# Inverse roots of the wide norms as exp(-ln/2) on ScalarE

## The reference

```
first block
  h = rmsnorm(x, norm_mix)                               ("mix")
  p = h @ w_in -> RWKV-7 (8 heads of 64), MLA (8 heads), differential attention (4 heads), gates
  RWKV:  kk = k*k_k / max(||k*k_k||, 1e-12) per head;  y = (y - mean) * rsqrt(var + 64e-5) per head
  MLA:   rmsnorm(c_q) over 256 ("q"), rmsnorm(c_kv) over 128 ("kv")
  diff:  rmsnorm(o, subln, eps=1e-5) over 128, per head   ("dsum")
  x = x + (gated sum of the three branches) @ w_o
  x = x + conv_ffn(rmsnorm(x, norm_ffn))                 ("ffn")
  x = rmsnorm(x, norm_final)                             ("fin")
second block, layers 0 and 1, modulated by silu(c) @ ada_w
  h = h + swiglu(modulate(rmsnorm(h)))                   ("s00", "s10")
  h = h + mixer(modulate(rmsnorm(h)))                    ("m0", "m1"; attention and a gMLP)
  h = h + swiglu(modulate(rmsnorm(h)))                   ("s01", "s11")
return rmsnorm(h, final_g)                               ("out")
rmsnorm(x, g) = x * rsqrt(mean(x*x) + 1e-6) * g
```

## Time and profile before

| | |
|---|---|
| three runs | 3799.27, 3800.09, 3807.25 us; median 3800.09 |
| profiled execution | 3798.57 us, its span 3796.8 us |
| busy, share of the span | PE 91%, PEld 72%, DVE 52%, ACT 34%, POOL 3% |
| granted clock of PE, mean | 0.955 |

### The profile page before, as it was taken

One profiled execution on the slowest core, in us unless ns is written; L12 is line 12 of the kernel. 1 busy time (PEld: TensorE's weight loads), 2 busy tenths in 40 slices (PEclk: granted clock), 3 DMA queues, 4 the chain that ended last, 5 costly groups with the idle time before them and its releaser, 6 DMA issues.

```text
span 3796.8 us, 46184 instructions
## 1 busy us (share of the span) xinstructions
PE 3445.9 (91%) x19472; PEld 2717.1 (72%) x19472; DVE 1960.4 (52%) x3248; ACT 1302.6 (34%) x2247; POOL 105.5 (3%) x202
## 2 busy tenths in 40 slices
PE   6888868999999899998789899999999878889998
PEld 4767736877888688866556688878887645677887
DVE  4665676667666665555544533343334454444333
ACT  3231456434434322224333322232223434333222
POOL 0000000010000011000000000000000000000000
PEclk8999979999999999999899999999999979999999
DMA  3010101454444365522011222222222200122221
GB/s 127 25 56 3 48 34 52 165 195 149 150 155 150 106 238 200 193 102 81 23 36 65 78 95 98 97 83 95 96 98 106 92 23 34 56 84 89 100 94 67
DMA packets 100543, 364.03 MB, mean 96 GB/s; under 512 B 11632, under 2 KB 11696, under 8 KB 99696
## 3 DMA queue, kind: packets, MB, share of 16 engines
q1 hardware_dynamic: 75888, 272.14, 19.8%
q0 software_dynamic: 24448, 88.95, 6.8%
HBM read 358.94 MB, written 2.10 MB: 95 GB/s over the span
## 4 chain that ended last, share of the span: by engine, by line
PE 80%; DVE 14%; ACT 4%; issue 1%; DMA 0%; DVEq 0%; POOL 0%; ACTq 0%; POOLq 0%
PE ps_run L397 79%; DVE wl L1660 1%; DVE nrm L1667 1%; PE ps_run L678 1%; DVE nP L1664 1%; DVE nrm L1670 1%; ACT nP L1021 1%; ACT wh L1021 1%; ACT nrm L1021 1%; DVE HL L1667 1%; DVE nst L1664 1%; DVE sq L1670 1%; DVE nst L2291 1%; ACT L1021 0%; DVE dP L1660 0%
## 5 line engine op out<-in xcount | busy, mean ns | idle before, releaser
L397 PE MATMUL ps_run<-HH,wh 128*128 128x512 f32 x2800 | 1137.9, 406 | 91.2 <-DVE HL L1667 48.9
L397 PE MATMUL ps_run<-HL,wh 128*128 128x512 f32 x2800 | 1109.2, 396 | 0.0
L397 PE MATMUL ps_run<-HH,wl 128*128 128x512 f32 x2800 | 1108.2, 396 | 0.0
L1660 DVE TENSOR_TENSOR wl<-st,wh 128x1024 fp32r<-128x1024 f32 x511 | 625.6, 1225 | 788.1 <-ACT wh L1021 787.6
L1021 ACT ACTIVATE wh<-st 128x1024 fp32r<-128x1024 f32 x511 | 538.3, 1054 | 749.5 <-PE ps_run L397 737.9
L397 PEld LDWEIGHTS ps_run<-HH,wh 128*128 128x128 f32 x2800 | 536.9, 192 | 231.1 <-DVE HL L1667 70.7
L397 PEld LDWEIGHTS ps_run<-HH,wl 128*128 128x128 f32 x2800 | 537.3, 192 | 115.7
L397 PEld LDWEIGHTS ps_run<-HL,wh 128*128 128x128 f32 x2800 | 538.9, 192 | 111.9 <-issue 6.9
L397 PE MATMUL ps_run<-AH,wh 128*128 128x512 f32 x1040 | 408.5, 393 | 0.0
L397 PE MATMUL ps_run<-AH,wl 128*128 128x512 f32 x1040 | 406.4, 391 | 0.0
L397 PE MATMUL ps_run<-AL,wh 128*128 128x512 f32 x1040 | 406.4, 391 | 0.0
(11 more groups left out here) (392 smaller groups left out, 3351.1 us busy)
## 6 DMA issues: line engine op xcount, KB each, us to landing
st<-wst SPq DMA_DIRECT2D x511, 512.0 KB, 3.2
mb<-ada POOLq DMA_DIRECT2D x144, 512.0 KB, 4.3
cw<-cw POOLq DMA_DIRECT2D x4, 1024.0 KB, 6.2
X<-xT SPq DMA_DIRECT2D x8, 256.0 KB, 10.0
X<-xT POOLq DMA_DIRECT2D x8, 256.0 KB, 5.4
out<-X SPq DMA_DIRECT2D x8, 256.0 KB, 2.1
kc<-kc POOLq DMA_DIRECT2D x1, 1137.5 KB, 7.3
mb<-cond POOLq DMA_DIRECT2D x2, 512.0 KB, 5.2
```

What stands on the lines that cost most here:

```text
L397: i = self.e.matmul(out, lhsT, rhs, start=start, stop=stop, skip_group_check=True)
L1660: self.e.tensor_tensor(out, a, b, op).then_inc(*self.w.done(*points))
```

## The change

The root and the reciprocal of every wide norm become two ScalarE instructions: Ln, which reads the sums from the bank with scale 1/dim and the epsilon as a bias, and Exp with scale -1/2. The three epsilons are three more columns of the constant table. The bank is freed by the Ln, and VectorE only waits for the result. In the norm of kk, VectorE bounds the sum by 1e-24 out of the bank, and ScalarE runs Ln and Exp on that. `table()` runs an Ln on its one column. The narrow roots and reciprocals stay. The diff, with repeated edits of the same kind left out:

```diff
@@ const_table
+    out["eps"] = np.tile(np.float32([1e-6, 1e-5, 64e-5]), (128, 1))
@@ Memory
+    def eps(self, eps):
+        i = (1e-6, 1e-5, 64e-5).index(eps)
+        return self.C("eps", i, i + 1)
@@ class Act
     def table(self):
-        self.act(self.m.junk, self.m.C("ones", 0, 1), ACT.Sqrt)
+        self.act(self.m.junk, self.m.C("ones", 0, 1), ACT.Ln)
-    def root(self, key, rs):
-        self.w.wait_ge("var", key)
-        self.act(rs, rs, ACT.Sqrt, ("std", key))
+    def inverse_root(self, rs, bank, dim, eps, inverse, *free):
+
+        self.act(rs, bank, ACT.Ln, *free, scale=1.0 / dim, bias=self.m.eps(eps))
+        self.w.own()
+        self.act(rs, rs, ACT.Exp, inverse, scale=-0.5)
+
+    def root(self, key, rs, dim=D):
+        self.w.wait_ge("sums", key)
+        self.inverse_root(rs, self.ps("sums", key), dim, 1e-6, ("inverse std", key), ("free", ("sums", key)))
@@ Act.rwkv_front
-        w.wait_ge(q, "nn")
-        self.act(s["sq"], self.ps((q, "nn")), ACT.Sqrt, ("free", (q, "nn")), (q, "norm"))
+        w.wait_ge(q, "nn bounded")
+        self.act(s["sq"], s["sq"], ACT.Ln)
+        w.own()
+        self.act(s["sq"], s["sq"], ACT.Exp, (q, "norm"), scale=-0.5)
@@ Act.rwkv_end
-        w.wait_ge(q, "y var")
-        self.act(s["sq"], s["sq"], ACT.Sqrt, (q, "y std"))
+        w.wait_ge(q, "var")
+        self.inverse_root(s["sq"], self.ps((q, "var")), 64, 64e-5, (q, "y std"), ("free", (q, "var")))
@@ Act.mla_prepared
-        self.root("q", m.mr)
+        self.root("q", m.mr, 256)
-        self.root("kv", m.mr)
+        self.root("kv", m.mr, 128)
@@ Act.merge_first
-                    w.wait_ge("dvar", h)
-                    self.act(m.nrm[2], m.nrm[2], ACT.Sqrt, ("dstd", h))
+                    w.wait_ge("dsum", h)
+                    self.inverse_root(m.nrm[2], self.ps("dsum", h), 128, 1e-5, ("dstd", h), ("free", ("dsum", h)))
@@ class Dve
-    def variance(self, key, dim, eps, rs):
-        self.w.wait_ge("sums", key)
-        self.ts(rs, self.ps("sums", key), 1.0 / dim, float(eps), MUL, ADD, ("free", ("sums", key)), ("var", key))
-
-    def root(self, key, dim, eps, rs):
-        self.variance(key, dim, eps, rs)
-        self.inverted(key, rs)
-
-    def inverted(self, key, rs):
-        self.w.wait_ge("std", key)
-        self.recip(rs, rs)
-        self.w.own()
+    def root(self, key):
+        self.w.wait_ge("inverse std", key)
@@ Dve.rwkv_front
         self.stt(s["kn"], s["kn"], 1.0, rk, ADD, MUL)
+        w.wait_ge(q, "nn")
+        self.ts(s["sq"], self.bank(q, "nn"), 1e-24, None, MAX, ("free", (q, "nn")), (q, "nn bounded"))
         next(fill)
         yield
         w.wait_ge(q, "norm")
-        self.ts(s["sq"], s["sq"], 1e-12, None, MAX)
-        w.own()
-        self.recip(s["sq"], s["sq"])
-        w.own()
         self.tt(s["kk"], s["kk"], s["sq"], MUL)
@@ Dve.rwkv_end
-        self.ts(s["sq"], self.bank(q, "var"), 1.0 / 64, 64e-5, MUL, ADD, ("free", (q, "var")), (q, "y var"))
         yield
         w.wait_ge(q, "y std")
-        self.recip(s["sq"], s["sq"])
-        w.own()
         self.tt(s["y"], s["y"], s["sq"], MUL)
@@ Dve.mla_prepared (kv alike)
-        self.variance("q", 256, 1e-6, m.mr)
-        yield
-        yield
-        self.inverted("q", m.mr)
+        yield
+        yield
+        self.root("q")
@@ Dve.merge_first
-                    w.wait_ge("dsum", h)
-                    self.ts(rs, self.ps("dsum", h), 1.0 / 128, 1e-5, MUL, ADD, ("free", ("dsum", h)), ("dvar", h))
                     w.wait_ge("dstd", h)
-                    self.recip(rs, rs)
-                    w.own()
                     self.tt(x, x, rs, MUL)
```

More of the change, by code:

```diff
@@ L1754, in first_norm @@
         self.tt(m.rl[:, 8:12].bitcast(F32R), m.rl[:, 0:4], m.rl[:, 4:8], SUB)
-        self.root("mix", D, 1e-6, m.nrm[2])
+        self.root("mix")
         self.scaled("mix", m.X, lambda i: m.V("norm_mix", i), m.nrm[2], m.nrm[3:6], m.HH, m.HL)
@@ L2034, in mla_prepared @@
         yield
-        self.variance("kv", 128, 1e-6, m.mr)
         yield
         yield
-        self.inverted("kv", m.mr)
+        self.root("kv")
         self.scaled("kv", [m.ckv], lambda i: m.V("kv_norm", i), m.mr, m.prep, m.MH[2:], m.ML[2:])
@@ L2162, in conv_ffn @@
         m, w = self.m, self.w
-        self.root("ffn", D, 1e-6, m.nrm[2])
+        self.root("ffn")
         w.wait_ge("pe ffn", "ffn", 0)
@@ L2198, in final_norm @@
         m = self.m
-        self.root("fin", D, 1e-6, m.nrm[2])
+        self.root("fin")
         for i in range(8):
@@ L2205, in adanorm @@
         mod = m.mod[l]
-        self.root(key, D, 1e-6, m.nrm[2])
+        self.root(key)
         self.scaled(key, m.X, lambda i: mod[:, 72 + 8 * sub + i:73 + 8 * sub + i], m.nrm[2], m.nrm[3:6], m.HH, m.HL,
@@ L2421, in program @@
         self.swiglu("s11", "out", 1, 2, iter(()))
-        self.root("out", D, 1e-6, m.nrm[2])
+        self.root("out")
         for i in range(8):
```

## The result

The kernel after took 3782.82 us (median of five runs, 3776.40 to 3786.34) against 3800.09 for before in the same comparison (five runs, 3795.92 to 3812.24): a ratio of 0.9945 [0.9924, 0.9966], where the brackets hold the 95% interval, as they do behind every ratio below. The forecast was 3770, with a range of 3752 to 3779. The direction is right; of the 30.4 us forecast, 17.3 came by the medians, 12.2 between the two profiled executions. The one of after took 3786.34 us, span 3784.6, granted clock 0.952.

What follows compares the result with a forecast made beforehand. TensorE mostly bounds the kernel, so the edit pays only where TensorE waits. Norms 19.0, fin 0.8, RWKV 4.9 and differential attention 5.7 sum to 30.4 us off 3798.57: 3768.2 profiled, 3770 as median, range 3752 to 3779.

Steps and rivals of the forecast that it cites:

- The chain of the norms: Norms over the model width: sums to scaling falls from 4.81 to 2.70 us, saving 2.11 each, 19.0 in nine.
- fin: The tenth model-width norm, where table loads for Silu and again for Ln intervene: a gain of 0.8 us.
- The placer: Table loads are picked for the function at hand, so a 1.28 us load stands between Ln and Exp; about 78 loads.
- the second rival: A table switch costs more right behind a wide instruction: at worst 17 us in all, 3787; half gives 3778; chance 0.07.
- RWKV: Norms of kk save 0.5 and 0.3 us, variances of y 2.7 and 1.4 in rounds one and two: 4.9 us.
- The first merge: Four norms (dsum) whose reciprocals TensorE's work covers, busy 49.90 of 50.10 us: the edit costed at nothing.
- The streams: RWKV rival: wl of the second fill comes too late and TensorE stops; some 5 us lost, 3775; chance 0.07.
- So an earlier start moves everything and costs no clock.: After each norm TensorE restarts at half clock and regains full clock before the last scaling tiles, so the saved time is kept.
- the differential attention: Norms q and kv, where VectorE sets the pace: MH moves up 2.6 and 1.6 us, kv's VectorE queue loses 1.5; 5.7 together.
- The bound of 8.5: Upper bound in us for the differential attention's gain, if TensorE's shorter stop spares it the half clock.

Runs made afterwards that it cites:

- ten norms alone: Against before, only the norms over the model width and table() changed; RWKV, q, kv and first merge kept root and reciprocal: 3787.29 us, ratio 0.9945.

## Why the prediction was wrong

**Right, to the size.** The chain of the norms: 2.70 us in "out", 2.11 saved in each; fin 0.78 for 0.8 (its first load at 1251.40, its first square at 1256.74; 5.34 us where the earlier trace rows has 6.12). The placer: 78 loads, one between every Ln and its Exp, at 1283 ns and with nothing behind a wide instruction, as the idle time of 2.1 us in front of all 78 shows; the second rival has no trace here. The drain of 1380 ns that the Trainium skill gives (ScalarE: Activation LUTs, "What ACT_TABLE_LOAD costs") doesn't show in this trace either: Ln ends at 3774.58, the load starts at 3774.60. RWKV: from the last square of the variances to the scaling by ln_w 10.5 us for 13.5 in round one (a gain of 3.0, forecast 2.7) and 9.3 for 10.6 in round two (1.3, forecast 1.4; against the earlier trace rows):

```profile
229.72 0.63 ACT L1026 ACTIVATE sq<-At 128x512 f32<-128x512 f32 x1 [1.96 <-DVE At L1680]
...
240.25 0.55 DVE L1677 TENSOR_SCALAR At<-At,vec 128x512 f32<-128x512 f32 x1
...
364.04 0.63 ACT L1026 ACTIVATE sq<-At 128x512 f32<-128x512 f32 x1 [0.23 <-DVE At L1680]
...
373.32 0.55 DVE L1677 TENSOR_SCALAR At<-At,vec 128x512 f32<-128x512 f32 x1
```

The first merge: 264.5 us with the MLA before it, before and after. The streams didn't starve: in round one TensorE has no wait for wl near 111 us, and waits 0.49 us for Bt (before 0.91). RWKV's part of its stage is 4.3 us of the 4.9 forecast, by the 392.7 us of ten norms alone against 388.4.

**Wrong: "So an earlier start moves everything and costs no clock."** This is the step that failed. It was read from the windows right behind one norm, where it holds, and was carried to everything behind. The SwiGLU stages bear it out: in each of the four behind fin, from the sums of the norm ahead of it to those of the norm behind, 373.2 to 373.4 us before and 371.1 to 371.4 after, the 2.11 of a norm. The mixers don't: TensorE's PEclk is 0.75 to 0.79 over 100 us of the first one, where it is busy for 75 to 78 of them, and how much of a mixer gets the full clock differs from profile to profile. Before's first mixer had 72 us at half clock; in after, 16 to 21 us earlier, it had 86 to 88, and with 0.63 us of idle copy 72 again. In the three profiles of after the two mixers take 792.5 to 797.7 us, in those of before 782.7 to 785.6: 7 to 15 us of the 30.4 went there, 14.8 between the forecast's own profile and the first of after. No term of the sum and no bound of the range covered this; a range that knew it would have been wider by that on its slow side. That another shift could as well have gained is not shown: no profile of any version has less half clock in its mixers than the least of before, 71.9 and 71.7 us.

**Mis-sized: the differential attention, 5.7 us.** It gave 1.1 us in two profiles of after and 2.9 in the third. The working asked what leaves VectorE's queue and counted its tensor_scalar as a gain; it didn't ask who waits for the bank that the tensor_scalar emptied. With the bank emptied by VectorE the stage gives 3.6 (one profile), inside the bounds of 3 and 8.5 but at their low end, so 2.1 us of the term are missing without the held bank, and no run isolates them. The bound of 8.5 counted on less half clock, and there was more: TensorE spends 53.2 to 53.4 us of the stage at it in before, 60.6 to 64.9 in after and 60.2 with the bank emptied.

**The comparison itself.** 17.3, 29.8 and 14.2 us are the three differences of medians for the same two kernels; after had 3782.8, 3779.4 and 3782.8, before 3800.1, 3809.1 and 3797.0. All nine runs of before in the second comparison lay at 3805 to 3813, and no profile of before was taken on that occasion, so why it was longer there stays open; that its mixers had more half clock is one guess, not shown. The second and third comparisons ran on different chips of the same kind, and after came out at 3779.4 and 3782.8 us on them. Open too is the second mixer: that its time goes with its half clock is seen in the table, but no run moved it alone. And the copy's effect on the first mixer rests on one profiled execution of each version.

## What to carry to other kernels

When an edit moves the work that empties a bank to another engine, ask who needs the bank next, and what stands in the new engine's queue ahead of it; let the engine that is there first empty it. When functions of two kinds alternate on ScalarE, look for the load between them in the trace and preload by hand the set that holds both: it was worth about as much here as the change itself, 19.7 us against 14 to 30. And where stages with many short stops of TensorE lie behind an edit, give the forecast some microseconds for each, on the slow side above all where the profile of before has little half clock in them, and take several profiles of both kernels before explaining a difference of that size.

## What the hardware showed

Work that does nothing can shorten a stage behind it: with one ScalarE copy of 0.63 us on the path, the first mixer of the profiled execution was 6.5 us shorter, with the same instructions and 15.6 us less at half clock, and the second 3.7 us shorter; the span was 11.1 us shorter (3781.2 to 3770.1). By the medians of six executions each the gain is 3.9 us and not clear of their spread. The first matmul of three profiles of before came at 14.4, 13.5 and 13.1 us, yet their first mixers agree within 0.2 us. The 78 table loads took 1283 ns in the mean, with 2.1 us of idle time ahead of all of them together.
